# Root columns interleaved with the value tiles, and one GpSimd split placed behind the first column

## The chip, the cores and the metric

The kernel runs on one core of one Trainium2 chip. Five engines work in it, each through its own list of instructions in order: PE (TensorE, matmuls; its weight loads are shown apart as PEld), DVE (VectorE), ACT (ScalarE), POOL (GpSimd) and SP (SyncE, which here only issues DMAs). They wait for one another by counting semaphores that the kernel places by hand. The metric is the device time of one execution in microseconds (us); lower is better.

## What is computed

One decoder block on 512 tokens of width 1024. The part that matters here is its beginning:

```python
h    = rms_norm(x, g_mix)                # x / sqrt(mean(x*x) + eps) * g
proj = h @ w_in                          # q_a,k_a,v_a | q_b,k_b,v_b | gate_a,gate_b
qa = rms_norm(heads(qa), q_norm_a); ka = rms_norm(heads(ka), k_norm_a)   # each of 64 columns
va = heads(va)                           # no norm of its own
```

Behind it stand block-sparse attention with 8 heads, sliding-window attention with 8 heads, two sigmoid gates, an output projection with residual, and a squared-relu feed-forward part.

## The kernel before

**Exact products from parts.** Every fp32 operand is split in a high part (fp32r) and a low part, the difference. A product of two such operands takes three matmuls: high by high, high by low, low by high. The weights come as slabs of 128 x 1024. For slab g, a DMA fills `w_raw`, ACT copies it to `w_hi` (`split_hi`, L624), POOL subtracts to get `w_lo` (`split_lo`, L534) and raises `w_lo_ready`, and PE then uses both. `w_hi` and `w_lo` have two places each, so the split of slab g+2 waits on PE's last use of slab g (`slab_done`).

**The value tiles.** The first four slabs hold the weights of v_a. PE computes them with tokens on partitions (L1476), into four accumulator banks, one for each 128 tokens (`va_tile(r)`, r = 0 to 3). These banks have to be scaled by 1 / rms of the token. That root is computed as a row that is equal on all partitions (`r_all`, 128 x 512), while the value tiles need it as a column, one value to a partition. `x_mean_square` on DVE ends with four `tensor_tensor_reduce` instructions (L1010): each multiplies 128 columns of `r_all` by the identity and sums, which leaves column r in `r_col`, and raises `r_col_ready`. In the profile each is a CUSTOM_DVE_ANT_0 and a DVE_READ_ACCUMULATOR2_ANT. Then ACT writes the scaled high part of tile r from its bank (`va_hi(r)`, L696), and DVE the low part (`va_lo(r)`, L1016), which needs `va_hi(r)`.

**What comes next.** The slabs 4 to 17 are the q and k slabs (13 of them) and v_b. PE does slab g into one of five banks in turn, `acc(g)`: 8 times three matmuls (L1375 to L1377). Slab 4 uses the free fifth bank. Slab 5 uses the bank of value tile 0, so before it PE waits for `w_lo_ready` of slab 5 and for `va_lo(0)`. Behind the matmuls of slab g stands the norm sum of slab g-1 (`head_norm_sum`, two matmuls, L1403 and L1404). It needs the squares of `acc(g-1)`: ACT writes them twice, as high part and in full (`qkv_square`, L660 and L661), and DVE subtracts to get their low part (`qk_split_squares`, L996). The bank's mean is read by DVE (`qk_mean`, L1027).

**Order around the change.** On ACT: `split_hi(5)`, the four `va_hi`, `split_hi(6)`, the squares of slab 4, `split_hi(7)`, and so on. On DVE: the root, the four columns, the four `va_lo`, then L996 of slab 4, L1027 of slab 4, L996 of slab 5. On POOL: `split_lo` of slabs 4, 5, 6, 7, then `split_lo` and `qk_split_lo` (L542) in turn.

Of the kernel before, what the change touches and what calls it, by code (L numbers as in the profile page):

```python
# [32 lines left out]
P = 128  # L33
KT = D // P
QT = S // P
# [56 lines left out]
def build(nc, x_t, slabs, params, table, onehot, tab_dram, out):  # L92
    F32, R = mybir.dt.float32, mybir.dt.float32r
    ALU, ACT = mybir.AluOpType, mybir.ActivationFunctionType
    ctx = ExitStack()
    with ctx:
        def sb(name, shape, dt):
            return ctx.enter_context(nc.sbuf_tensor(name, shape, dt))
# [7 lines left out]
        def sem(name):  # L106
            return ctx.enter_context(nc.semaphore(name))
# [24 lines left out]
        r_all = sb("r_all", [P, S], F32)  # L132
        ident = sb("ident", [P, P], F32)
# [6 lines left out]
        r_col = softmax[:, 0, 0:QT]  # L140
        diagonal = store[:, 12, 0:P]
# [81 lines left out]
        r_col_ready = sem("r_col_ready")  # L223
# [36 lines left out]
        def qk_count(slab):  # L260

            return sum(kind in "qk" for kind in QKV_KIND[:slab])
# [26 lines left out]
        def key_tiles(i, qt):  # L289

            nk = min(2, qt + 1) if i < 8 else qt + 1
            return qt + 1 - nk, nk
# [3 lines left out]
        def units(step):  # L296

            p, qt = step // QT, QT - 1 - step % QT
            return [(2 * step + e, 2 * p + e, e, qt) for e in range(2)]
# [219 lines left out]
        @block.gpsimd  # L519
        def _(pool):  # L520
            pool.memset(ident[:, :], 0.0).then_inc(ident_ready, 1)
            pool.wait_ge(ident_ready, 1)
            pool.affine_select(out=ident[:, :], in_=ident[:, :], compare_op=ALU.not_equal, fill=1.0,
                               base=0, pattern=[[-1, P]], channel_multiplier=1).then_inc(ident_ready, 1)

            pool.wait_ge(arrived[0], 16)
            pool.wait_ge(w_hi_ready, 1)
            pool.tensor_scalar(w_hi[:, 0, FIRST * P:D], w_raw[:, 0, FIRST * P:D], 1.0, 0.0,
                               ALU.mult, ALU.add).then_inc(w_hi_ready, 1)

            def split_lo(g, count):

                pool.wait_ge(w_hi_ready, count)
                pool.tensor_tensor(w_lo[:, g % WS, :], w_raw[:, g % RAW, :],  # L534
                                   w_hi[:, g % WS, :].bitcast(F32), ALU.subtract).then_inc(w_lo_ready, 1)


            def qk_split_lo(g):

                t, n = QKV_TILE[g], qk_count(g)  # L540
                pool.wait_ge(qk_hi_ready, n + 1)
                pool.tensor_tensor(qk_lo[:, t, :], pre[n % 2], qk_hi[:, t, :].bitcast(F32),  # L542
                                   ALU.subtract).then_inc(qk_lo_ready, 1)

            def normalise(step):

                for u, i, e, qt in units(step):
                    n = P * key_tiles(i, qt)[1]
                    pool.wait_ge(rec_ready, step + 1)
                    pool.tensor_scalar(probs[:, u % 4, 0:n], probs[:, u % 4, 0:n], rec[:, u % 8:u % 8 + 1], 1.0,  # L550
                                       ALU.mult, ALU.mult).then_inc(probs_ready, 1)

            def y_lo(p):

                pool.wait_ge(y_hi_ready, p + 1)
                pool.tensor_tensor(qk_lo[:, y_tile(p), :], y_both[:, :], qk_hi[:, y_tile(p), :].bitcast(F32),
                                   ALU.subtract).then_inc(y_lo_ready, 1)

            pool.wait_ge(w_lo_ready, 3)
            for s in range(4, G_GATE + 2):  # L560
                split_lo(s, s + 3)

                if s - 4 >= N_VA:
                    qk_split_lo(s - 4)
            for step in range(STEPS + 1):
                if step >= 1:
                    normalise(step - 1)
                if step == 4:
                    qk_split_lo(LAST_Q)
                if step >= 3 and step % 2:  # L570
                    s = G_GATE + 2 + (step - 3) // 2
                    split_lo(s, s + 3)
                if step >= 8 and step % 4 == 0:
                    y_lo(step // 4 - 2)
            split_lo(G_BRANCH + 1, G_BRANCH + 4)
            split_lo(LATE + 1, LATE + 4)
            for g in range(LATE + 2, G_FF + 3):
                split_lo(g, g + 3)

            def up_lo(j, c):  # L580

                split_lo(G_FF + j, c * TILES + (G_FF + j + 3))

            def down_lo(k, c):

                from_, high, low = unit_at(k, c)
                pool.wait_ge(unit_hi_ready, unit_count(k, c))
                pool.tensor_tensor(low, from_, high.bitcast(F32), ALU.subtract).then_inc(b_lo_ready, 1)

            def chunk_lows(c):  # L590

                down_lo(0, c)
                up_lo(3, c)
                up_lo(4, c)
                down_lo(3, c)
                up_lo(5, c)
                up_lo(6, c)
                down_lo(5, c)

            def last_lows(c):  # L600

                down_lo(0, c)
                up_lo(3, c)
                pool.wait_ge(s_ready, c * 4 + 4)
                down_lo(2, c)
                pool.wait_ge(u_lo_ready, u_count(2, c))
                down_lo(3, c)
                down_lo(4, c)
                pool.wait_ge(u_lo_ready, u_count(3, c))
                down_lo(5, c)  # L610

            with pool.Fori(0, CHUNKS - 1) as c:
                chunk_lows(c)
            last_lows(CHUNKS - 1)

        @block.scalar
        def _(act):
# [19 lines left out]
            for k in range(KT):  # L637
                if k == 0:
                    hi_part(0, slice(0, FIRST * P), first_arrived[0])
                if k == 4:  # L640
# [5 lines left out]
                               scale=par[:, C_MIX + k:C_MIX + k + 1]).then_inc(x_hi_ready, 1)  # L646
# [45 lines left out]
            def va_hi(r):  # L692

                act.wait_ge(slab_done, N_VA)
                act.wait_ge(r_col_ready, QT)
                act.activation(va_hi_part[r], va_tile(r), ACT.Copy,  # L696
                               scale=r_col[:, r:r + 1]).then_inc(va_hi_ready, 1)

# [5 lines left out]
            for r in range(QT):  # L704
                va_hi(r)
# [100 lines left out]
            for n in range(N_OUT):  # L806
# [3 lines left out]
                               scale=par[:, C_FFN + n:C_FFN + n + 1]).then_inc(x1_hi_ready, 1)  # L810
# [107 lines left out]
        def _(dve):  # L918
# [30 lines left out]
            for k in range(KT):  # L949
# [4 lines left out]
                if k == 4:  # L954
# [4 lines left out]
                                         scalar=par[:, C_MIX + k:C_MIX + k + 1],  # L959
                                         in1=x_hi[:, k, :].bitcast(F32), op0=ALU.mult,  # L960
                                         op1=ALU.subtract).then_inc(x_lo_ready, 1)
# [37 lines left out]
            def x_mean_square():  # L999
                dve.wait_ge(ms_done, 1)  # L1000
                dve.tensor_scalar(r_inv_sq, bank[5][:, :], EPS, None, ALU.add).then_inc(ms_ready, 1)
                dve.wait_ge(r_root_ready, 3)
                refine(r_all[:, :], r_root, r_root_sq, r_inv_sq, r_ready, 2)
                dve.wait_ge(ident_ready, 2)
                dve.wait_ge(r_ready, 2)
                dve.wait_ge(xsum_lo_ready, 1)
                for r in range(QT):
                    if r:
                        dve.wait_ge(r_col_ready, r)
                    dve.tensor_tensor_reduce(out=diagonal, in0=r_all[:, P * r:P * r + P], in1=ident[:, :], scale=1.0,  # L1010
                                             scalar=0.0, op0=ALU.mult, op1=ALU.add,
                                             accum_out=r_col[:, r:r + 1]).then_inc(r_col_ready, 1)

            def va_lo(r):
                dve.wait_ge(va_hi_ready, r + 1)
                dve.scalar_tensor_tensor(out=va_lo_part[r], in0=va_tile(r), scalar=r_col[:, r:r + 1],  # L1016
                                         in1=va_hi_part[r].bitcast(F32), op0=ALU.mult,
                                         op1=ALU.subtract).then_inc(va_lo_ready, 1)
# [50 lines left out]

            x_mean_square()  # L1070
            for r in range(QT):
                va_lo(r)
            for g in range(N_VA, N_QKV):
                if g in (10, 11):
# [104 lines left out]
            for n in range(N_OUT):  # L1179
# [7 lines left out]
                                         scalar=par[:, C_FFN + n:C_FFN + n + 1],  # L1187
                                         in1=qk_hi[:, n, :].bitcast(F32), op0=ALU.mult,
                                         op1=ALU.subtract).then_inc(x1_lo_ready, 1)
# [156 lines left out]
            for m in range(2):  # L1346
# [6 lines left out]
                                     in1=to[:, part], op0=ALU.mult, op1=ALU.add).then_inc(rest_sum_ready, 1)  # L1353
# [5 lines left out]
            for h, part in enumerate(HALVES):  # L1359
# [3 lines left out]
                else:  # L1363
                    dve.wait_ge(half_done, 1)
                dve.scalar_tensor_tensor(out=to[:, part], in0=product[:, part], scalar=factor(2, 1), in1=to[:, part],
                                         op0=ALU.mult, op1=ALU.add).then_inc(out_ready, 1)
# [450 lines left out]
```

## Time and profile before

| what | us |
|---|---|
| median of 3 runs | 677.76 |
| lowest and highest | 677.14, 677.97 |
| span of the profiled execution | 674.9 |
| PE busy | 668.8 (99%) |
| DVE busy | 504.8 (75%) |
| ACT busy | 370.2 (55%) |
| POOL busy | 322.9 (48%) |

The span reaches from the first to the last instruction. The profile gives no other time for its execution; the median of the runs is 2.9 us above its span, which lies outside of the first and last instruction. "Busy" is time in which the engine worked on at least one instruction; PE's ends are modelled from the pipeline, so the start times of its rows tell more than the durations. The mean granted TensorE clock over the span is 1.000 of full.

### The profile page before, as it was taken

Reading aid. Unit: us, or ns where it says so; the run is one execution under the profiler, and the core shown is the slowest. Engines: PE = TensorE matmul, PEld = TensorE weight load, DVE = VectorE, ACT = ScalarE, POOL = GpSimd, SP = SyncE. Lnnn points to the kernel's source line nnn. Section 1 sums busy time; section 2 is a strip of 40 time slices with the busy share of each in tenths; the row PEclk is TensorE's granted clock in tenths of the full one; section 3 lists DMA queues with packets and bytes.
Section 4 is the critical chain, followed back from the end, with each engine's and each line's share of the span. In section 5 each row is a group of like instructions: output and inputs, shape, how many; then the busy total and the mean of one; then the engine's idle time right before and its main releaser. Section 6 shows DMA issues by size and latency. Waiting matters only on the chain.

```text
span 674.9 us, 9472 instructions
## 1 busy us (share of the span) xinstructions
PE 668.8 (99%) x3238; PEld 553.7 (82%) x3238; DVE 504.8 (75%) x701; ACT 370.2 (55%) x662; POOL 322.9 (48%) x194
## 2 busy tenths in 40 slices
PE   9999999999999999999999999999999999999998
PEld 7878787788888888888888888888888888888886
DVE  6667898555555555785559879788797888978897
ACT  7467676676665566543347546254463525536360
POOL 0246676456556653444446436246352454435532
PEclk9999999999999999999999999999999999999999
DMA  8222242222232213555222232414132151220303
GB/s 320 95 93 94 76 128 82 78 81 93 96 94 75 71 45 113 157 181 188 82 93 93 100 118 65 153 62 154 64 113 104 62 186 62 93 101 25 125 0 125
DMA packets 22909, 69.87 MB, mean 104 GB/s; under 512 B 2731, under 2 KB 4011, under 8 KB 22876
## 3 DMA queue, kind: packets, MB, share of 16 engines
q1 hardware_dynamic: 22588, 68.92, 30.3%
q10 hardware_dynamic: 288, 0.52, 0.2%
q8 instruction: 19, 0.31, 0.2%
q14 instruction: 14, 0.11, 0.1%
HBM read 67.27 MB, written 2.16 MB: 103 GB/s over the span
## 4 chain that ended last, share of the span: by engine, by line
PE 94%; DVE 2%; ACT 2%; issue 1%; DMA 1%; POOL 0%; SPq 0%; DVEq 0%; ACTq 0%
PE bank L1375 20%; PE bank L1377 20%; PE bank L1376 20%; PE bank L1692 8%; PE bank L1689 8%; PE bank L1691 8%; PE bank L1476 3%; PE bank L1538 2%; PE bank L1525 2%; PE bank L1559 1%; PE bank L1561 1%; DMA store<-x_t 1%; PE bank L1661 1%; DVE store L1010 0%; PE bank L1404 0%
## 5 line engine op out<-in xcount | busy, mean ns | idle before, releaser
L534 POOL TENSOR_TENSOR w_lo<-w_raw,w_hi 128x1024 fp32r<-128x1024 f32 x77 | 190.2, 2474 | 232.7 <-ACT w_hi L624 232.7
L1375 PE MATMUL bank<-qk_hi,w_hi 128*128 128x512 f32 x320 | 125.0, 391 | 0.0
L1377 PE MATMUL bank<-qk_hi,w_lo 128*128 128x512 f32 x320 | 124.5, 389 | 0.0
L1376 PE MATMUL bank<-qk_lo,w_hi 128*128 128x512 f32 x320 | 124.5, 389 | 0.0
L1375 PE MATMUL bank<-x_hi,w_hi 128*128 128x512 f32 x304 | 122.4, 403 | 1.6 <-DVE v_parts L1016 1.1
L1377 PE MATMUL bank<-x_hi,w_lo 128*128 128x512 f32 x304 | 118.8, 391 | 0.0
L1376 PE MATMUL bank<-x_lo,w_hi 128*128 128x512 f32 x304 | 118.4, 389 | 0.0
L624 ACT ACTIVATE w_hi<-w_raw 128x1024 fp32r<-128x1024 f32 x80 | 83.9, 1056 | 59.4 <-PE bank L1377 55.0
L1258 DVE SCALAR_TENSOR_TENSOR store<-bank,softmax,store 128x512 f32<-128x512 f32 x101 | 72.0, 744 | 23.2 <-PE bank L1692 23.1
L1692 PE MATMUL bank<-v_parts,x_lo 128*128 128x512 f32 (+1 forms) x218 | 84.4, 387 | 0.0
L1689 PE MATMUL bank<-v_parts,x_hi 128*128 128x512 f32 (+1 forms) x218 | 84.4, 387 | 0.0
L1377 PEld LDWEIGHTS bank<-qk_hi,w_lo 128*128 128x128 f32 x320 | 60.1, 188 | 12.6
L1375 PEld LDWEIGHTS bank<-qk_hi,w_hi 128*128 128x128 f32 x320 | 60.1, 188 | 12.4 <-DVE w_lo L1169 0.2
L1376 PEld LDWEIGHTS bank<-qk_lo,w_hi 128*128 128x128 f32 x320 | 60.1, 188 | 12.3
L1375 PEld LDWEIGHTS bank<-x_hi,w_hi 128*128 128x128 f32 x304 | 57.1, 188 | 13.8 <-issue 2.9
L1377 PEld LDWEIGHTS bank<-x_hi,w_lo 128*128 128x128 f32 x304 | 57.0, 188 | 12.5
L1376 PEld LDWEIGHTS bank<-x_lo,w_hi 128*128 128x128 f32 x304 | 57.2, 188 | 10.8
L550 POOL TENSOR_SCALAR probs<-probs,softmax 128x256 f32<-128x256 f32 (+3 forms) x64 | 31.3, 502 | 58.8 <-DVE softmax L1106 58.8
L1111 DVE TENSOR_TENSOR pt_lo<-bank,pt_hi 128x256 fp32r<-128x256 f32 (+3 forms) x64 | 27.9, 439 | 35.8 <-ACT pt_hi L747 35.5
L836 ACT ACTIVATE v_parts<-qk_lo_again 128x1024 fp32r<-128x1024 f32 x21 | 21.5, 1056 | 56.2 <-DVE qk_lo_again L1201 44.9
L1692 PEld LDWEIGHTS bank<-v_parts,x_lo 128*128 128x128 f32 x218 | 40.9, 188 | 8.4
L1689 PEld LDWEIGHTS bank<-v_parts,x_hi 128*128 128x128 f32 x218 | 40.9, 188 | 8.3
(165 smaller groups left out, 1213.1 us busy)
## 6 DMA issues: line engine op xcount, KB each, us to landing
w_raw<-slabs SPq DMA_DIRECT2D x80, 512.0 KB, 3.3
bias_m<-slabs SPq DMA_DIRECT2D x16, 512.0 KB, 3.6
qk_hi_again<-slabs SPq DMA_DIRECT2D x16, 512.0 KB, 5.2
store<-x_t SPq DMA_DIRECT2D x16, 256.0 KB, 3.4
bias_m<-tab_dram SPq DMA_DIRECT2D x8, 256.0 KB, 4.3
out<-store SPq DMA_DIRECT2D x7, 256.0 KB, 2.1
bias_m<-tab_dram SPq DMA_DIRECT2D x8, 128.0 KB, 3.6
w_raw<-slabs ACTq DMA_DIRECT2D x2, 256.0 KB, 3.4
```

The source lines that it names most:

```text
L534: pool.tensor_tensor(w_lo[:, g % WS, :], w_raw[:, g % RAW, :], w_hi[:, g % WS, :].bitcast(F32), ALU.subtract).then_inc(w_lo_ready, 1)
L550: pool.tensor_scalar(probs[:, u % 4, 0:n], probs[:, u % 4, 0:n], rec[:, u % 8:u % 8 + 1], 1.0, ALU.mult, ALU.mult).then_inc(probs_ready, 1)
L624: act.activation(w_hi[:, g % WS, :], w_raw[:, g % RAW, :], ACT.Copy).then_inc(w_hi_ready, 1)
L836: act.activation(high, from_, ACT.Copy).then_inc(unit_hi_ready, 1)
L1111: dve.tensor_tensor(pt_lo[:, slot(u), keys], bank[5 + e][:, keys], pt_hi[:, slot(u), keys].bitcast(F32), ALU.subtract).then_inc(pt_lo_read ...
L1258: dve.scalar_tensor_tensor(out=to, in0=product, scalar=factor(j, m), in1=to, op0=ALU.mult, op1=ALU.add).then_inc(ready, 1)
L1375: pe.matmul(out_, wh, xh, start=first, stop=False)
L1376: pe.matmul(out_, wh, xl, start=False, stop=False)
L1377: last = pe.matmul(out_, wl, xh, start=False, stop=end)
L1689: pe.matmul(to, u_high, high[:, p, cols], start=(opens and p == 0), stop=False, skip_group_check=True)
L1691: pe.matmul(to, u_high, low[:, p, cols], start=False, stop=False, skip_group_check=True)
L1692: last = pe.matmul(to, u_low, high[:, p, cols], start=False, stop=(p == 1), skip_group_check=True)
```

## The change

Three things. In DVE's list, `r_column(r)` is cut out of `x_mean_square` and stands ahead of `va_lo(r)` in the loop over tiles. ACT's `va_hi(r)` waits for r+1 columns and no longer for all four. POOL's `split_lo(5)` waits for the first column.

```diff
--- before
+++ after
@@ gpsimd @@
             pool.wait_ge(w_lo_ready, 3)
             for s in range(4, G_GATE + 2):
+                if s == 5:
+                    pool.wait_ge(r_col_ready, 1)
                 split_lo(s, s + 3)
@@ scalar @@
             def va_hi(r):
                 act.wait_ge(slab_done, N_VA)
-                act.wait_ge(r_col_ready, QT)
+                act.wait_ge(r_col_ready, r + 1)
@@ vector @@
                 dve.wait_ge(xsum_lo_ready, 1)
-                for r in range(QT):
-                    if r:
-                        dve.wait_ge(r_col_ready, r)
-                    dve.tensor_tensor_reduce(... accum_out=r_col[:, r:r + 1]).then_inc(r_col_ready, 1)
+
+            def r_column(r):
+
+                if r:
+                    dve.wait_ge(r_col_ready, r)
+                dve.tensor_tensor_reduce(... accum_out=r_col[:, r:r + 1]).then_inc(r_col_ready, 1)
@@ vector @@
             x_mean_square()
             for r in range(QT):
+                r_column(r)
                 va_lo(r)
```

DVE's list before, from the end of the root to the first squares of a q or k slab. An ISA row that writes `store` is a column's reduction, the one that writes `softmax` alone its read of the sum; bank0, 1, 2 and 6 are the value tiles 0 to 3.

```order
L984 SCALAR_TENSOR_TENSOR r_all<-store 128x512 [waits r_root_ready]
L987 SCALAR_TENSOR_TENSOR r_all<-r_all,store 128x512 [waits r_ready]
L1010 ISA store,softmax<-r_all,ident 128x128 [waits xsum_lo_ready,r_ready,ident_ready]
L1010 ISA softmax 128x1
L1010 ISA store,softmax<-r_all,ident 128x128 [waits r_col_ready]
...
L1016 SCALAR_TENSOR_TENSOR v_parts<-bank0,softmax,v_parts 128x8x64 [waits va_hi_ready]
L1016 SCALAR_TENSOR_TENSOR v_parts<-bank1,softmax,v_parts 128x8x64 [waits va_hi_ready]
L1016 SCALAR_TENSOR_TENSOR v_parts<-bank2,softmax,v_parts 128x8x64 [waits va_hi_ready]
L1016 SCALAR_TENSOR_TENSOR v_parts<-bank6,softmax,v_parts 128x8x64 [waits va_hi_ready]
L996 TENSOR_TENSOR pt_lo<-store,pt_hi 128x512 [waits sq_ready]
```

The same stretch of DVE's list now:

```order
L1014 ISA store,softmax<-r_all,ident 128x128 [waits xsum_lo_ready,r_ready,ident_ready]
L1014 ISA softmax 128x1
L1020 SCALAR_TENSOR_TENSOR v_parts<-bank0,softmax,v_parts 128x8x64 [waits va_hi_ready]
L1014 ISA store,softmax<-r_all,ident 128x128 [waits r_col_ready]
...
L1020 SCALAR_TENSOR_TENSOR v_parts<-bank1,softmax,v_parts 128x8x64 [waits va_hi_ready]
...
L1020 SCALAR_TENSOR_TENSOR v_parts<-bank6,softmax,v_parts 128x8x64 [waits va_hi_ready]
L998 TENSOR_TENSOR pt_lo<-store,pt_hi 128x512 [waits sq_ready]
```

The four columns stood in a row ahead of the four low parts; each of the last three columns now stands behind the low part of the tile before it, and with it behind that tile's wait for ACT.

POOL's list at its splits of slabs 4 to 7, as a difference:

```order
 L528 TENSOR_SCALAR w_hi<-w_raw 128x512 [waits w_hi_ready,slab_arrived0]
 L534 TENSOR_TENSOR w_lo<-w_raw,w_hi 128x1024 [waits w_hi_ready,w_lo_ready]
-L534 TENSOR_TENSOR w_lo<-w_raw,w_hi 128x1024 [waits w_hi_ready] x4
+L534 TENSOR_TENSOR w_lo<-w_raw,w_hi 128x1024 [waits w_hi_ready,r_col_ready]
+L534 TENSOR_TENSOR w_lo<-w_raw,w_hi 128x1024 [waits w_hi_ready] x3
 L542 TENSOR_TENSOR qk_lo<-store,qk_hi 128x512 [waits qk_hi_ready]
```

Nothing moved there; the second split of the four, slab 5's, has one wait more. The lists of PE and ACT hold the same instructions in the same order, and SP's list is unchanged.

## Rows read from the trace of the kernel before

**Rows 1.** The page, part 1: busy us, share of the span, count.

```profile
PE 668.8 (99%) x3238; PEld 553.7 (82%) x3238; DVE 504.8 (75%) x701; ACT 370.2 (55%) x662; POOL 322.9 (48%) x194
```

**Rows 2.** Waits of PE: who waited for whom, total us, times, longest us.

```profile
PE bank L1375 <- DVE v_parts L1016: 1.1, 1, 1.1
```

**Rows 3.** Timeline of DVE: start, duration, line, operation, count, [idle before <- releaser].

```profile
30.55 2.27 DVE L1010 CUSTOM_DVE_ANT_0 store<-r_all,ident 128x128 f32<-128x128 f32 x1
...
32.86 0.29 DVE L1010 CUSTOM_DVE_ANT_0 store<-r_all,ident 128x128 f32<-128x128 f32 x1
33.08 0.08 DVE L1010 DVE_READ_ACCUMULATOR2_ANT softmax<- 128x1 f32 x1
...
33.75 0.08 DVE L1010 DVE_READ_ACCUMULATOR2_ANT softmax<- 128x1 f32 x1
34.65 2.73 DVE L1016 SCALAR_TENSOR_TENSOR v_parts<-bank,softmax,v_parts 128x512 fp32r<-128x512 f32 x4 [0.81 <-ACT v_parts L696]
38.31 2.01 DVE L996 TENSOR_TENSOR pt_lo<-store,pt_hi 128x512 fp32r<-128x512 f32 x1 [0.93 <-ACT store L661]
```

**Rows 4.** Timeline of POOL.

```profile
30.23 2.45 POOL L534 TENSOR_TENSOR w_lo<-w_raw,w_hi 128x1024 fp32r<-128x1024 f32 x1 [3.47 <-ACT w_hi L624]
37.38 2.39 POOL L534 TENSOR_TENSOR w_lo<-w_raw,w_hi 128x1024 fp32r<-128x1024 f32 x1 [4.71 <-ACT w_hi L624]
...
48.38 2.41 POOL L534 TENSOR_TENSOR w_lo<-w_raw,w_hi 128x1024 fp32r<-128x1024 f32 x1 [3.47 <-ACT w_hi L624]
50.75 1.74 POOL L542 TENSOR_TENSOR qk_lo<-store,qk_hi 128x512 fp32r<-128x512 f32 x1
...
60.17 2.41 POOL L534 TENSOR_TENSOR w_lo<-w_raw,w_hi 128x1024 fp32r<-128x1024 f32 x1 [1.79 <-ACT w_hi L624]
...
117.60 1.29 POOL L542 TENSOR_TENSOR qk_lo<-store,qk_hi 128x512 fp32r<-128x512 f32 x1
```

**Rows 5.** Timeline of DVE, two further instructions that ran beside POOL.

```profile
49.31 2.03 DVE L996 TENSOR_TENSOR pt_lo<-store,pt_hi 128x512 fp32r<-128x512 f32 x1 [0.98 <-ACT store L661]
...
60.83 0.68 DVE L1027 SCALAR_TENSOR_TENSOR store<-store,bank 128x512 f32<-128x512 f32 x1
```

**Rows 6.** Timeline of ACT.

```profile
29.09 1.06 ACT L624 ACTIVATE w_hi<-w_raw 128x1024 fp32r<-128x1024 f32 x1
33.93 2.42 ACT L696 ACTIVATE v_parts<-bank,softmax 128x512 fp32r<-128x512 f32 x4 [3.78 <-DVE softmax L1010]
36.23 1.08 ACT L624 ACTIVATE w_hi<-w_raw 128x1024 fp32r<-128x1024 f32 x1
...
37.65 0.62 ACT L661 ACTIVATE store<-bank 128x512 f32<-128x512 f32 x1
```

**Rows 7.** Timeline of PE around slab 5 (matmuls).

```profile
34.04 0.39 PE L1377 MATMUL bank<-x_hi,w_lo 128*128 128x512 f32 x1
35.55 0.47 PE L1375 MATMUL bank<-x_hi,w_hi 128*128 128x512 f32 x1 [1.12 <-DVE v_parts L1016]
35.85 0.40 PE L1376 MATMUL bank<-x_lo,w_hi 128*128 128x512 f32 x1
36.09 0.39 PE L1377 MATMUL bank<-x_hi,w_lo 128*128 128x512 f32 x1
...
41.09 0.39 PE L1403 MATMUL bank<-pt_hi,pt_lo 128*128 128x512 f32 x1
...
41.54 0.39 PE L1375 MATMUL bank<-x_hi,w_hi 128*128 128x512 f32 x1
```

**Rows 8.** Timeline of PE in the first 10 us.

```profile
0.93 4.63 PE L1450 MATMUL bank<-ones 128*128 128x128 f32 x20 [0.93 <-DVE ones L919]
5.91 1.68 PE L1476 MATMUL bank<-w_hi,x_hi 128*128 128x512 f32 x4 [0.34 <-ACT x_hi L645]
7.43 1.08 PE L1476 MATMUL bank<-w_lo,x_hi 128*128 128x512 f32 x4
```

**Rows 9.** One window: busy us of each engine (count), granted clock, DMA share, GB/s.

```profile
34.00:42.00 8.00, 6.88 (x31) 5.37 (x31) 5.00 (x6) 4.93 (x8) 2.39 (x1) 1.00 0.30 101
```

More of the change, by code:

```diff
@@ L1006, in x_mean_square @@
                 dve.wait_ge(xsum_lo_ready, 1)
-                for r in range(QT):
-                    if r:
-                        dve.wait_ge(r_col_ready, r)
-                    dve.tensor_tensor_reduce(out=diagonal, in0=r_all[:, P * r:P * r + P], in1=ident[:, :], scale=1.0,
-                                             scalar=0.0, op0=ALU.mult, op1=ALU.add,
-                                             accum_out=r_col[:, r:r + 1]).then_inc(r_col_ready, 1)
+            def r_column(r):
+                if r:
+                    dve.wait_ge(r_col_ready, r)
+                dve.tensor_tensor_reduce(out=diagonal, in0=r_all[:, P * r:P * r + P], in1=ident[:, :], scale=1.0,
+                                         scalar=0.0, op0=ALU.mult, op1=ALU.add,
+                                         accum_out=r_col[:, r:r + 1]).then_inc(r_col_ready, 1)
             def va_lo(r):
```

## The prediction

> **What bounds the kernel now.** I read the busy shares first: PE is busy 99% of the span [rows 1]. So an edit to DVE, ACT and POOL moves the time only where PE waits for them. The list of PE's waits, read second, has one entry that belongs to the edited lines: PE stood 1.1 us ahead of slab 5 until `va_lo(0)` was done [rows 2]. Everything else in this stretch must be judged by how close it is to making PE wait. For that I laid the timelines of the four engines from 28 to 42 us beside each other.
>
> **Why PE waits there.** ACT had slab 5's high part at 29.09 + 1.06 = 30.15, and POOL began its low part at 30.23 [rows 4, 6]. DVE began the first column at 30.55. That reduction lasted 2.27 us, the next one, of the same form, 0.29 [rows 3]. It ended at 32.82, which is 0.14 behind POOL's end (30.23 + 2.45 = 32.68). The same pattern stands at L996: its two sources lie in SBUF, it began at 38.31 inside POOL's work of 37.38 to 39.77 and ended at 40.32, 0.55 behind it [rows 3, 4]; once more, 49.31 + 2.03 = 51.34 against POOL's 48.38 + 2.41 = 50.79, again 0.55 [rows 4, 5]. L1027, with one source in SBUF and one in a bank, took 0.68 wholly inside POOL's 60.17 to 62.58 [rows 4, 5]. I read this as: a DVE instruction with two SBUF sources waits for the running POOL instruction and then does its own work (0.14 us for 128 columns, 0.55 for 512); one that reads a bank does not wait.
>
> The Trainium skill names such a lock (SBUF — State Buffer, section "Who interferes with whom"): with two SBUF inputs DVE contends with a GpSimd instruction that reads SBUF, and whoever comes first keeps the port for its whole instruction. It speaks of instruction classes and not of this custom reduction. Its rule gives the first column 0.29 us once POOL is held back, and also speaks against the change, since column 1 then meets POOL; a cost of first use, the rival below, would leave the 2.27 us where they are.
>
> **What the change removes.** POOL now starts behind column 0, so column 0 should take 0.29 us: its sum is read out at about 30.55 + 0.30 = 30.85 (0.30 from the start of a reduction to the end of its read, 32.86 to 33.16 in [rows 3]). ACT started `va_hi(0)` 0.10 behind the last read (33.83 to 33.93) and DVE `va_lo(0)` 0.72 later (34.65) [rows 3, 6]. So `va_hi(0)` starts at 30.95, `va_lo(0)` at 31.67 and is over by 32.4. POOL starts slab 5's low part 0.08 behind its release, as it did behind ACT (30.15 to 30.23), at 30.93, and with 2.45 us ends at 33.38. PE's last matmul of slab 4 starts at 34.04 and the next could start 0.23 later, at 34.27 [rows 7]. Both conditions of slab 5 are met by then, with 0.9 us to spare. The stall of 1.12 us goes, and with it the slow restart: the steps behind it were 0.30 and 0.24 us where the steady one is 0.227 (22 steps from 36.09 to 41.09), so 0.09 more. Slab 5's 24 matmuls then end, and the norm sum of slab 4 could start, at 34.27 + 24 x 0.227 = 39.71, against 41.09 before: **1.38 us earlier**. This would be the whole gain.
>
> **What is late next.** The columns 1 to 3 are no longer free. DVE goes from `va_lo(0)` to column 1 at 31.67 + 0.66 = 32.33 (four `va_lo` in 2.73 us: steps of 0.66). POOL is now in slab 5's low part until 33.38, so column 1 waits: it ends at 33.38 + 0.14 and is read by 33.53. From there each round is a relay between two engines: 0.10 to ACT, 0.72 to `va_lo`, 0.66 to the next column, 0.30 to its read, 1.78 us in all. Column 2 is read at 35.31, column 3 at 37.09, `va_hi(3)` starts at 37.19. Before, ACT started `split_hi(6)` at 36.23; its four `va_hi` ran in a row from 33.93 to 36.35, so the last began near 35.66, 0.57 before [rows 6]. Now `split_hi(6)` starts at 37.19 + 0.57 = **37.76, later by 1.53 us**.
>
> Behind it, in ACT's order, stand the squares of slab 4, and behind these PE's norm sum. Before: `split_hi(6)` 36.23, POOL's split of slab 6 37.38 (1.15 later) to 39.77, the square L661 37.65 (1.42 later), L996 38.31 (0.66 behind that), its end 40.32. PE came to the norm sum at 41.09 and did not wait; a release takes 0.16 to reach PE (`va_lo(0)` 34.65 + 0.74 = 35.39, PE 35.55), so 41.09 - 40.48 = 0.6 us was the slack [rows 3, 4, 6, 7]. Now: POOL has slab 6 from 38.91 to 41.30, L661 starts at 39.18, L996 starts at 39.84, inside POOL's instruction, and ends at 41.30 + 0.55 = 41.85. PE can start the norm sum at **42.01**. It gets there at 39.71 and stands for 2.3 us.
>
> **The sum.** The norm sum is at 42.01 against 41.09, +0.92; the slow restart, 0.09, moves with the stall, and adds as PE goes on to slab 6: 41.54 becomes 42.55, **+1.0 us**. So one stall of 1.12 us is traded for one of 2.3 us. It doesn't come back later: slab 6's low part is ready at 41.30 and `va_lo(1)` at 34.3 + 0.8 = 35.1, both before PE needs them; ACT's `split_hi(7)` waits on PE's last use of slab 5, which comes earlier, so POOL has slab 7's low part by some 44.2, where PE needs it at 42.55 + 26 x 0.227 = 48.5. From slab 6 on the other engines wait for PE in each slab, and the program is as before, only shifted. SP's loads are behind `w_lo_ready` of four slabs before: slab 9's and slab 10's loads go out 0.7 and 1.5 us later, and ACT takes these slabs up only behind PE's slabs 7 and 8, some 20 us on at 26 x 0.227 = 5.9 us a slab, so they cost nothing. The added POOL wait costs nothing beyond the shift counted: behind it only the split of slab 6 is queued, which waits for ACT longer. The span becomes 675.9; with the 2.9 us outside, from the median 677.76, the time is **678.8 us**, +0.15%. That is inside the 0.2% (1.4 us) which a measurement of this kernel can just tell from none.
>
> **Rivals.**
>
> *Column 1 isn't held up* (a short reduction slips in, or POOL starts late enough). Then column 1 starts at 32.33 and is read by 32.63, all behind it is 0.90 earlier, L996 ends at 40.95, PE starts the norm sum at 41.11 instead of 41.09, with the restart 0.1 later than before: 677.9. Against it: each of the three two-SBUF instructions above waited to POOL's end. Chance 0.12.
>
> *The 2.27 us are the first use of the custom reduction*, not POOL. It is the first such instruction of the program, so the row alone fits both. Then POOL's split of slab 5 is pushed to 32.9, ends at 35.4, and every step above is 1.98 later: +3.0, 680.8. Against it stands that it ended 0.14 behind POOL, as the lock asks. Chance 0.06.
>
> *POOL goes first at 41.30.* L996 waits for slab 6's low part, and POOL's slab 7 part is released by ACT by then. If POOL takes it up ahead of L996, that one waits a further 2.4: +3.4, 681.2. Against it: at 50.79 POOL had its next instruction ready, and DVE went first; that POOL instruction took 1.74 us where a lone one took 1.29, 0.45 of waiting [rows 4, 5]. Chance 0.05.
>
> *The clock falls.* Over the window with the 1.12 us stall the granted clock stayed 1.00 [rows 9]; no longer stall is in the trace, and the new one is twice that. At the start PE ran at the lower level: four matmuls took 1.68 us, the next four 1.08 [rows 8], 0.6 lost. If the lower level lasted as long as from PE's first matmul to there (0.93 to 7.43, 6.5 us), half of it would be lost, 3.2. So +1.6 to +4.2: 679.4 to 682.0. Chance 0.09. The Trainium skill (TensorE: Matmul & The Clock Gate, "What's actually happening") says that idleness halves TensorE's clock until activity releases it; the trace's stall of 1.12 us did not do this.
>
> *The gain stays.* If L996 were not held (POOL and DVE not in each other's way) and ACT's relay shorter than I reckon, PE reaches the norm sum unhindered: -1.4, 676.4. It needs L996's end by 39.55, while its start alone is at 39.84, or 38.94 with column 1 free. Chance 0.06.
>
> **How the numbers follow.** My forecast, the traded stall, has 0.62 and its own range 678.1 to 679.6 (0.3 us on the relay's hand-offs, 0.4 on a median). The range 677.2 to 681.0 takes in the forecast, the free column, the first use and the lower half of the clock's case, about 0.82. Slower by over 0.2% (above 679.1): a quarter of the forecast, 0.15, first use 0.06, POOL first 0.05, clock 0.08: 0.34. Faster by over 0.2%: most of the last rival, 0.05. The rest, 0.61, is within.
>
> **What would show it.** In the changed kernel's timeline: the first L1014 reduction at 0.29 us, POOL's L534 right behind it at about 30.9, the second reduction at over 1 us; no wait of PE ahead of slab 5 and a wait of about 2.3 us on L998's product ahead of the norm sum, now L1408; ACT's `split_hi(6)` near 37.8. The forecast is wrong if PE's list of waits has nothing at the norm sum, if the first reduction stays above 2 us, or if matmuls behind the stall step at 0.43 us.

## The result, and the profile after

| | before | changed |
|---|---|---|
| median, 15 runs each | 676.92 us | 679.07 us |
| lowest and highest | 676.23, 678.87 | 676.88, 680.54 |
| ratio | | 1.0021, 95% interval 1.0011 to 1.0031 |
| span of the profiled execution | 674.9 us | 675.9 us |
| TensorE clock, mean of each run | 0.999 or 1.000 in all of the 72 runs taken beside the experiments | 0.999 or 1.000 in 8 runs, 0.996 or 0.997 in 7 |

The changed kernel is slower by 0.2%, 1.4 us with an interval of 0.7 to 2.1. The plain difference of the two medians is larger, 2.15 us; I go by the ratio and its interval. The profiled execution of it, at clock 1.000, has the span of the forecast, 675.9 us. The median is a little above the forecast's 678.8, and inside the range.

PE's list of waits in the changed kernel (who waited for whom, total us, times, longest):

```profile
PE bank L1408 <- DVE pt_lo L998: 2.0, 1, 2.0
```

The wait ahead of slab 5 [rows 2] is gone, and one at the norm sum has come. DVE's timeline shows why; it answers to [rows 3]:

```profile
30.62 0.29 DVE L1014 CUSTOM_DVE_ANT_0 store<-r_all,ident 128x128 f32<-128x128 f32 x1
...
31.74 0.75 DVE L1020 SCALAR_TENSOR_TENSOR v_parts<-bank,softmax,v_parts 128x512 fp32r<-128x512 f32 x1 [0.82 <-ACT v_parts L698]
32.41 1.15 DVE L1014 CUSTOM_DVE_ANT_0 store<-r_all,ident 128x128 f32<-128x128 f32 x1
33.49 0.08 DVE L1014 DVE_READ_ACCUMULATOR2_ANT softmax<- 128x1 f32 x1
34.38 0.75 DVE L1020 SCALAR_TENSOR_TENSOR v_parts<-bank,softmax,v_parts 128x512 fp32r<-128x512 f32 x1 [0.82 <-ACT v_parts L698]
35.05 0.28 DVE L1014 CUSTOM_DVE_ANT_0 store<-r_all,ident 128x128 f32<-128x128 f32 x1
...
37.03 0.08 DVE L1014 DVE_READ_ACCUMULATOR2_ANT softmax<- 128x1 f32 x1
37.93 0.75 DVE L1020 SCALAR_TENSOR_TENSOR v_parts<-bank,softmax,v_parts 128x512 fp32r<-128x512 f32 x1 [0.82 <-ACT v_parts L698]
39.85 1.99 DVE L998 TENSOR_TENSOR pt_lo<-store,pt_hi 128x512 fp32r<-128x512 f32 x1 [1.17 <-ACT store L663]
```

The first column takes 0.29 us, the second meets GpSimd and takes 1.15, and the low parts come one by one, 0.82 us of waiting for ACT ahead of each, where they stood in one row of four before. ACT gets to its copy of slab 6 late by that, at 37.80 where it was 36.23:

```profile
37.80 1.05 ACT L626 ACTIVATE w_hi<-w_raw 128x1024 fp32r<-128x1024 f32 x1
```

GpSimd's timeline, which answers to [rows 4]:

```profile
31.00 2.41 POOL L534 TENSOR_TENSOR w_lo<-w_raw,w_hi 128x1024 fp32r<-128x1024 f32 x1 [4.17 <-DVE softmax L1014]
38.93 5.17 POOL L534 TENSOR_TENSOR w_lo<-w_raw,w_hi 128x1024 fp32r<-128x1024 f32 x2 [5.51 <-ACT w_hi L626]
```

Slab 6's low part starts at 38.93 where it started at 37.38. L998 came at 39.85, inside it, and ended at 41.84. The two GpSimd instructions in a row took 5.17 us where twice 2.41 is 4.82: the second waited for L998. PE's timeline, which answers to [rows 7]:

```profile
39.55 0.39 PE L1382 MATMUL bank<-x_hi,w_lo 128*128 128x512 f32 x1
41.90 0.50 PE L1408 MATMUL bank<-pt_hi,pt_lo 128*128 128x512 f32 x1 [1.96 <-DVE pt_lo L998]
42.23 0.39 PE L1409 MATMUL bank<-pt_lo 128*128 128x512 f32 x1
42.47 0.40 PE L1380 MATMUL bank<-x_hi,w_hi 128*128 128x512 f32 x1
```

From the first column's start to slab 6's first matmul it is 42.47 - 30.62 = 11.85 us, before it was 41.54 - 30.55 = 10.99: **0.86 us later**. This difference, "column to slab 6", is what I compare the experiments by. It leaves out what happens ahead of the columns, where the start of an execution varies by half a us and more with the arrival of x.

### The profile page after: what moved, and what is told of

It reads as the page before. It is cut to its first block, busy times and chain, and to the rows that moved or that the text cites. A ratio compares the mean times of both kernels' runs of the same rounds, so it can differ in the third digit from the quotient of the medians.

```text
span 675.9 us, 9473 instructions
## 1 busy us (share of the span) xinstructions
PE 668.9 (99%) x3238; PEld 553.7 (82%) x3238; DVE 503.0 (74%) x701; ACT 370.8 (55%) x662; POOL 323.6 (48%) x194
## 4 chain that ended last, share of the span: by engine, by line
PE 93%; ACT 2%; DVE 2%; issue 1%; DMA 1%; POOL 0%; SPq 0%; ACTq 0%; DVEq 0%
PE bank L1380 20%; PE bank L1382 20%; PE bank L1381 20%; PE bank L1694 8%; PE bank L1697 8%; PE bank L1696 8%; PE bank L1481 3%; PE bank L1543 2%; PE bank L1530 2%; PE bank L1564 1%; PE bank L1566 1%; DMA store<-x_t 1%; PE bank L1666 1%; PE bank L1408 0%; PE bank L1409 0%
```

## The experiments

### The changed kernel again, and with its stall filled

The first question was the part of the 1.4 us that the 0.9 of the trace does not give. Two kernels ran on one chip: the changed kernel itself, and the changed kernel with work of no use in the stall:

```diff
+FILL = 9
...
+                    if (g, kt) == (5, KT - 1):
+                        for _ in range(FILL):
+                            pe.matmul(bank[4][:, :], x_hi[:, 0, 0:P], x_hi[:, 1, :], start=True, stop=True)
                     if (g, kt) in AFTER:
```

> The changed kernel once more, to see its runs with their spans and granted clocks beside those of the kernel before. Theory A (only the traded stall, PE waits 2.0 us at the norm sum in the place of 1.1 us ahead of slab 5): all runs lie about 1.0 us over the kernel before, ratio 1.0015, and the mean granted clock is 1.000 in each. Theory B (the longer stall also lets TensorE's clock fall in part of the runs): runs at 1.000 lie 1.0 us over before, and runs at about 0.997 lie some 2 us higher still (0.003 of 676 us is 2.0), ratio 1.002 to 1.003.

> The changed kernel, with nine more matmuls of 512 columns (their result is not used) on PE between slab 5 and the norm sum of slab 4: 9 x 0.227 = 2.04 us of work in the place of the 1.96 us that PE stands there. No other engine's work changes. Both theories: the norm sum still starts near 41.9 us and the profile's span stays at 675.9 us, within 0.2. Theory A: the timed runs are as the changed kernel's, ratio to it within 0.05%. Theory B: with the stall filled the granted clock is 1.000 in every run and the median falls by 1 to 1.5 us against the changed kernel, to 1.0 us over before.

Measured: the kernel before 677.65 us on this chip; the changed kernel 679.48, ratio to before 1.0028 (1.0016 to 1.0040), 2 of its 6 runs at a mean clock of 0.997, these two with a median of 679.86, the four at 1.000 with 679.04. In the first table the eight runs at 0.999 or more have a median of 678.2, 1.3 us over before, and the seven lower ones 679.6. So a lower mean clock adds some 0.8 to 1.4 us to the runs that have it, less than the 2 of Theory B. With the stall filled it is 677.44, ratio 1.0002 (0.9994 to 1.0011), all 12 runs at 0.999 or 1.000. PE's timeline with the stall filled:

```profile
39.26 2.20 PE L1511 MATMUL bank<-x_hi 128*128 128x512 f32 x9
41.42 0.50 PE L1409 MATMUL bank<-pt_hi,pt_lo 128*128 128x512 f32 x1
41.76 0.40 PE L1410 MATMUL bank<-pt_lo 128*128 128x512 f32 x1
41.99 0.39 PE L1381 MATMUL bank<-x_hi,w_hi 128*128 128x512 f32 x1
```

The first column starts at 30.10 there, 0.5 us earlier than in the profile of the changed kernel, and the span, 675.5, is shorter by about as much. Column to slab 6 is 11.89 us: the program is as late as the changed kernel, 0.90 over before, and still its runs are 2.0 us shorter than the changed kernel's in the median, where Theory B had 1 to 1.5, and level with before where it had 1.0 over. PE did nothing more useful in that time; it was only not idle. The part of this that the runs name is the clock: no run with the stall filled shows a mean below 0.999. The lower means alone, though, stand in fewer than half of the changed kernel's runs, and so don't carry 2.0 us.

### The new order without GpSimd's wait

```diff
             for s in range(4, G_GATE + 2):
-                if s == 5:
-                    pool.wait_ge(r_col_ready, 1)
                 split_lo(s, s + 3)
```

> The changed kernel without GpSimd's new wait: columns interleaved with the tiles, GpSimd takes slab 5's low part at 30.2 us as before. My relay: column 0 is held to GpSimd's end and read at 32.83, columns 1 to 3 free at 34.61, 36.39, 38.17; ACT's slab 6 copy at 38.84, GpSimd's slab 6 part 39.99 to 42.39, the low squares of slab 4 end at 42.94, PE's norm sum at 43.1. So PE waits about 0.3 us ahead of slab 5 and 3.0 us at the norm sum, and slab 6 starts 2.1 us later than before: span 677.0. A rival, that the hold-up is counted once in either order and the two are alike, gives 675.9. If the clock falls with a longer stall, the runs at a lower clock are more than in the changed kernel, and their median is above 679.5.

Measured: 681.06 us, ratio to before 1.0051 (1.0033 to 1.0069), 5 of 6 runs at 0.994 to 0.997; profiled span 679.2. PE's timeline, and then three windows of 2 us (busy us of PE, PEld, DVE, ACT and POOL with counts, granted clock, DMA share, GB/s):

```profile
42.35 0.80 PE L1406 MATMUL bank<-pt_hi,pt_lo 128*128 128x512 f32 x1 [2.65 <-DVE pt_lo L996]
42.95 0.63 PE L1407 MATMUL bank<-pt_lo 128*128 128x512 f32 x1
43.37 0.63 PE L1378 MATMUL bank<-x_hi,w_hi 128*128 128x512 f32 x1
...
48.06 0.62 PE L1380 MATMUL bank<-x_hi,w_lo 128*128 128x512 f32 x1
48.49 0.43 PE L1378 MATMUL bank<-x_hi,w_hi 128*128 128x512 f32 x1
48.76 0.40 PE L1379 MATMUL bank<-x_lo,w_hi 128*128 128x512 f32 x1
```

```profile
40.00:42.00 2.00, 0.00 (x0) 0.00 (x0) 1.68 (x1) 2.00 (x4) 2.00 (x2) 0.93 0.00 0
42.00:44.00 2.00, 1.65 (x4) 1.36 (x5) 0.69 (x2) 0.21 (x1) 2.00 (x1) 0.50 0.58 190
...
46.00:48.00 2.00, 2.00 (x6) 1.59 (x5) 1.61 (x3) 0.28 (x1) 0.00 (x0) 0.50 0.51 195
```

After 2.65 us of idleness the granted clock is 0.50, the 1.2 GHz level, and a matmul steps on every 0.43 us in the place of 0.227. It is 14 steps from 42.35 to 48.49, 6.14 us where 14 x 0.227 is 3.18: 3.0 us lost, restart included. The relay itself came out as reckoned: the first column took 2.27 us, the norm sum started 42.35 - 29.99 = 12.36 us behind the first column, 1.82 over the 10.54 of before (2.0 was forecast). That the first column is back at 2.27 us with GpSimd's wait taken out, and was 0.29 with it in, ties its length to GpSimd; the rival by which the two orders cost the same has fallen. This is the clearest view of the rival that I had priced at 0.6 to 3.2 us and given a chance of 0.09.

### GpSimd behind all four columns, columns in a row

The kernel before with two lines:

```diff
             for s in range(4, G_GATE + 2):
+                if s == 5:
+                    pool.wait_ge(r_col_ready, 4)
                 split_lo(s, s + 3)
```

> The kernel before with one edit: GpSimd takes slab 5's low part behind all four columns; the columns stay in a row. The four columns then take 0.34 each and are read by 31.9; ACT's four parts run from 32.0, GpSimd's slab 5 part from 32.0 to 34.4, PE starts slab 5 at 34.5 (0.25 us of waiting in the place of 1.12). ACT's slab 6 copy is then bound by PE's end of slab 4, 34.5, GpSimd's slab 6 part ends at 38.1, the low squares of slab 4 at 38.7, well ahead of PE's norm sum at 40.0. So the whole program is 1.0 us earlier: span 673.9, ratio 0.9985. The rival, that slab 5's low part coming later costs as much as the held column, gives 674.9.

Measured: 676.48 us, ratio to before 0.9986 (0.9977 to 0.9995), clock 1.000 in all 11 runs, span 673.3 (673.9 was forecast; the first column came 0.7 us earlier than in the profile of before). DVE's, GpSimd's and PE's timelines:

```profile
29.85 0.29 DVE L1012 CUSTOM_DVE_ANT_0 store<-r_all,ident 128x128 f32<-128x128 f32 x1
...
30.86 0.29 DVE L1012 CUSTOM_DVE_ANT_0 store<-r_all,ident 128x128 f32<-128x128 f32 x1
31.07 0.08 DVE L1012 DVE_READ_ACCUMULATOR2_ANT softmax<- 128x1 f32 x1
31.97 2.73 DVE L1018 SCALAR_TENSOR_TENSOR v_parts<-bank,softmax,v_parts 128x512 fp32r<-128x512 f32 x4 [0.82 <-ACT v_parts L698]
```

```profile
31.24 2.40 POOL L534 TENSOR_TENSOR w_lo<-w_raw,w_hi 128x1024 fp32r<-128x1024 f32 x1 [4.95 <-DVE softmax L1012]
```

```profile
33.69 0.50 PE L1377 MATMUL bank<-x_hi,w_hi 128*128 128x512 f32 x1
...
39.72 0.39 PE L1377 MATMUL bank<-x_hi,w_hi 128*128 128x512 f32 x1
```

All four columns are read 1.3 us behind the start of the first. GpSimd comes at 31.24 and hinders none of them; PE stands some 0.1 us ahead of slab 5. Column to slab 6 is 39.72 - 29.85 = 9.87 us, 1.12 less than before. The same wait that the change adds for one column pays when it stands behind four, with the columns left together.

### GpSimd's wait for one column alone

The same two lines with `1` in the place of `4`.

> The kernel before with GpSimd's wait alone: slab 5's low part behind the first column, the four columns in a row and ACT waiting for all four, as before. Column 0 takes 0.29 us. GpSimd is released 0.08 behind its read, when DVE has just begun column 1 (0.11 behind the read), so the engines meet between columns. Theory D (a waiting instruction gets the port before the next one of the engine that just had it, as at 50.79 us in the profile before): GpSimd goes in behind column 1, columns 2 and 3 wait 2.4 us, the last read is at 34.1 against 33.83 before, and the program is 0.2 us later: span 675.1, ratio 1.000 to 1.001. Rival (DVE keeps the port for its row of columns): all four are read by 32, as in four_columns, and the program gains 1.0 us: 673.9, ratio 0.9985.

Measured: 677.93 us against 677.54, ratio 1.0006 (0.9994 to 1.0017); span 676.2, where 675.1 was forecast, about 1 us more, which comes up again at the end of the experiments. DVE's, GpSimd's and PE's timelines:

```profile
30.04 0.29 DVE L1012 CUSTOM_DVE_ANT_0 store<-r_all,ident 128x128 f32<-128x128 f32 x1
...
30.37 0.29 DVE L1012 CUSTOM_DVE_ANT_0 store<-r_all,ident 128x128 f32<-128x128 f32 x1
...
30.71 2.36 DVE L1012 CUSTOM_DVE_ANT_0 store<-r_all,ident 128x128 f32<-128x128 f32 x1
```

```profile
30.42 2.50 POOL L534 TENSOR_TENSOR w_lo<-w_raw,w_hi 128x1024 fp32r<-128x1024 f32 x1 [3.92 <-DVE softmax L1012]
```

```profile
35.12 0.47 PE L1377 MATMUL bank<-x_hi,w_hi 128*128 128x512 f32 x1 [1.21 <-DVE v_parts L1018]
```

GpSimd went in between columns 1 and 2, and column 2 took the 2.3 us that column 0 took before. PE waits 1.2 us ahead of slab 5 and slab 6 starts 41.12 - 30.04 = 11.08 us behind the first column, 0.1 later than before. The engine that waits gets in at the next gap, as expected; the wait alone moves the hold-up from one column to another.

### The squares ahead of slab 6's copy

The changed kernel with ACT's `qkv_square(4)` put ahead of `split_hi(6)`:

```diff
             for g in range(N_VA, N_QKV):
+                if g == 4:
+                    qkv_square(g)
                 split_hi(g + 2)
...
-                if not is_v(g):
+                if not is_v(g) and g > 4:
                     qkv_square(g)
```

> The changed kernel with ACT's two squares of slab 4 ahead of its copy of slab 6. Then DVE's L998 starts near 38.9, before GpSimd has slab 6, takes 0.69 and the norm sum follows at 39.8 without a wait. If GpSimd's hold on L998 were what costs the 2.0 us, the program would gain them. My sum says that slab 6's low part is late by nearly as much: ACT's copy 38.8 to 39.8, GpSimd 39.9 to 42.3, PE at 42.45 on slab 6 where the changed kernel had 42.47. So the 2.0 us wait moves from the norm sum to slab 6 and nothing is gained: span 675.9 at clock 1.000.

Measured: 678.65 us against 677.54, ratio 1.0013 (1.0003 to 1.0022), 4 of 10 runs at 0.997; span 676.8. DVE's low squares and PE:

```profile
38.22 0.69 DVE L1000 TENSOR_TENSOR pt_lo<-store,pt_hi 128x512 fp32r<-128x512 f32 x1 [0.22 <-ACT store L663]
```

```profile
39.31 0.39 PE L1411 MATMUL bank<-pt_lo 128*128 128x512 f32 x1
41.62 0.50 PE L1382 MATMUL bank<-x_hi,w_hi 128*128 128x512 f32 x1 [1.92 <-POOL w_lo L534]
```

The low squares take 0.69 us, and PE waits 1.92 us for GpSimd's low part of slab 6 instead. Column to slab 6 is 41.62 - 29.93 = 11.69, 0.70 over before. So with GpSimd's hold on the squares gone, only 0.16 us is won. The test is not a clean one, as the squares in front make the copy of slab 6 later themselves; but in the kernel before and in the one with GpSimd behind four columns L996 and L998 were held just as long (2.01 and 2.02 us), and PE did not wait for them. What costs is the relay that makes ACT late for both of its jobs, the squares and slab 6. The granted clock fell to 0.5 in this profile too, three matmuls behind the restart: nine steps, from 42.42 to 46.07, took 3.65 us where 9 x 0.227 is 2.04, 1.6 us lost. The span is yet only 0.9 over the 675.9 that I had written for clock 1.000, because the first column started 0.7 us earlier than in the changed kernel's profile.

### The start, and the two edits together

In the second profile of the changed kernel (span 678.5 us) PE waited 1.33 us at the mean square, which no other profile shows:

```profile
24.22 2.85 DVE L982 TENSOR_TENSOR pt_hi<-store,pt_hi 128x512 fp32r<-128x512 f32 x1
```

```profile
24.15 2.37 POOL L534 TENSOR_TENSOR w_lo<-w_raw,w_hi 128x1024 fp32r<-128x1024 f32 x1 [18.37 <-ACT w_hi L626]
```

It is the same meeting, at slab 4. To keep it out, one line puts slab 4's low part behind the last step of the sum of squares:

```diff
             pool.wait_ge(w_lo_ready, 3)
+            pool.wait_ge(xsum_lo_ready, 1)
```

This line went into the kernel before, the changed kernel, the one with the stall filled, and the one with GpSimd behind four columns.

> The kernel before, with GpSimd's low part of slab 4 put behind DVE's x_sum_lo (the last step of the sum of squares, two SBUF sources). In a profiled execution of the changed kernel that step met GpSimd's slab 4 part by a hair (24.22 against 24.15), lasted 2.85 us and made PE wait 1.33 us at the mean square; in the profile of before it was over first (23.19). Theory C (this chance meeting at the start makes the two groups of times that the kernel before shows, near 676.5 and 677.8): no run has it any more, the runs lie in one group at 676.2 to 677.0, median about 0.7 us under before where half of its runs are in the upper group. Rival (the two groups come from elsewhere): ratio within 0.03% of before, groups unchanged.

> The changed kernel with the same edit at the start. If the change's own cost is the traded stall plus a clock that falls in part of the runs, this lies over before_start by 1.0 us in the runs at clock 1.000 and by some 3 us in those at 0.997: median 1.0 to 3.0 us over before_start.

> The changed kernel with the edit at the start and the nine unused matmuls in the stall ahead of the norm sum. With the start's lottery taken out, the traded stall alone is left: 0.9 to 1.0 us over before_start (ratio between the two 1.0014), clock 1.000 in all runs. The first filled kernel came out at 1.0002 of before, less than the 1.0015 of this sum; if the sum is wrong, this one will be level with before_start again.

> The kernel before with GpSimd's slab 4 part behind x_sum_lo and its slab 5 part behind all four columns (columns in a row, as before): both edits keep GpSimd off a DVE step that PE waits for. 1.0 us from slab 5, and what before_start brings: about 675.3, ratio to before 0.997 to 0.998, and the lowest of all.

| kernel, with the line at the start | us, median | ratio to before (677.39) | runs at 0.997 |
|---|---|---|---|
| before | 677.85 | 1.0008 (0.9997 to 1.0020) | 0 of 12 |
| changed | 678.90 | 1.0026 (1.0014 to 1.0037) | 4 of 8 |
| changed, stall filled | 677.09 | 1.0000 (0.9991 to 1.0009) | 0 of 11 |
| behind four columns | 675.45 | 0.9972 (0.9961 to 0.9983) | 0 of 8 |

My theory on the start fell: the kernel before gained nothing by the line, and its runs spread as before, from 676.48 to 678.32 with one at 680.82. The meeting at slab 4 is real, but it stands in one of the eight profiles taken without the line, too rare to make the spread. The changed kernel with the line is 1.05 us over the kernel before with it, inside the 1.0 to 3.0 forecast; with the stall filled it is 0.8 under it, where 0.9 to 1.0 over was forecast. The last kernel met its forecast of 675.3 in number, though the part of it that the line was to bring isn't there. The changed kernel's profile of this set has the clock's fall at the changed kernel's own stall. PE's timeline and two windows:

```profile
41.38 0.50 PE L1409 MATMUL bank<-pt_hi,pt_lo 128*128 128x512 f32 x1 [1.96 <-DVE pt_lo L999]
...
42.18 0.49 PE L1382 MATMUL bank<-x_lo,w_hi 128*128 128x512 f32 x1
...
42.89 0.63 PE L1381 MATMUL bank<-x_hi,w_hi 128*128 128x512 f32 x1
43.32 0.63 PE L1382 MATMUL bank<-x_lo,w_hi 128*128 128x512 f32 x1
...
45.83 0.40 PE L1382 MATMUL bank<-x_lo,w_hi 128*128 128x512 f32 x1
```

```profile
42.00:44.00 2.00, 2.00 (x7) 1.56 (x6) 1.86 (x2) 1.10 (x2) 1.58 (x1) 0.59 0.58 225
44.00:46.00 2.00, 2.00 (x6) 1.57 (x6) 1.24 (x3) 0.79 (x2) 0.00 (x0) 0.56 0.71 205
```

The stall is 1.96 us, as in the profile above that stayed at 1.00; here the clock fell about 1 us behind the restart (the mean of 0.59 over 42 to 44 puts the step near 42.4). From 42.18 to 45.83 it is nine steps, 3.65 us where 9 x 0.227 is 2.04: 1.6 us lost.

The last kernel is the fastest of all: 0.28% under the kernel before. In its profile column to slab 6 is 39.96 - 30.10 = 9.86 us, 1.13 less than before. The interval runs from 1.15 to 2.6 us less; the trace's 1.13 lies at its edge, and the median's 1.9 us is more than the trace gives.

**One source of the spread of the runs** shows in that same profile, whose execution (676.48 us) was the slowest of its kernel's 8; the other seven lie from 675.05 to 675.48. DVE near the end, in the last chunk of the feed-forward part, and GpSimd beside it:

```profile
636.35 1.23 DVE L1204 TENSOR_TENSOR qk_lo_again<-qk_hi_again,qk_lo_again 128x1024 f32<-128x1024 f32 x1 [1.75 <-DMA qk_hi_again<-slabs]
637.49 3.43 DVE L1208 TENSOR_TENSOR bias_m<-qk_hi_again,bias_m 128x1024 f32<-128x1024 f32 x1
```

```profile
636.66 3.18 POOL L534 TENSOR_TENSOR w_lo<-w_raw,w_hi 128x1024 fp32r<-128x1024 f32 x1 [3.47 <-ACT w_hi L627]
```

```profile
654.55 0.47 PE L1692 MATMUL bank<-w_hi,x_hi 128*128 128x512 f32 x1 [0.52 <-issue]
```

DVE had waited 1.75 us for a DMA; in the profile of 673.3 us above it waited 0.97, began L1207 before GpSimd came, and that step took 1.22. Here the step fell behind GpSimd and took 3.43. It is a third place of the same meeting, decided by when one DMA lands, and PE waits twice behind it, 0.8 us in all. Three of the twelve profiles (this one, the second of the changed kernel and that of the wait alone) show DVE waiting 1.66 us or more for this DMA, and in all three a step of DVE then falls behind GpSimd. From slab 6's first matmul to the end of the span it is 634.7 to 635.1 us in these three, and 633.3 to 633.8 in the six others whose clock stayed at 1.00: the meeting costs 0.9 to 1.8 us. The two groups in which the runs of the kernel before lie, near 676.5 and 677.8, are about as far apart; that this meeting makes them isn't shown, since a timed run leaves no trace. I have not tried to take it out.

## Why the prediction was right, point by point

- **The bound.** Right: only PE's waits counted, and the change replaced one by another.
- **Column 0 without GpSimd: 0.29 us.** Measured 0.29. It is also the first use of the custom reduction, so the rival that blamed the first use has fallen; so has the one by which column 1 isn't held, since it took 1.15 us.
- **The relay.** Forecast: column 1 read at 33.53, `va_hi(3)` 37.19, `split_hi(6)` 37.76, the low squares 39.84 to 41.85. Measured, with the first column 0.07 later than before: read at 33.57, ACT's copy of slab 6 at 37.80, the low squares 39.85 to 41.84. The round of 1.78 us was measured at 1.77 (two rounds from 33.49 to 37.03 between reads).
- **Who goes first at GpSimd's end.** Right: DVE, and GpSimd's slab 7 part waited 0.35 us. With L998 held and the relay as long as forecast, the rival by which the gain stays has fallen too. The kernel with the wait alone shows the mirror image, GpSimd going in ahead of DVE's next column.
- **The stall, 2.3 us.** By the forecast's own count, from the start that was possible to the one that was made, it is 41.90 - (39.55 + 0.23) = 2.1 us; the profile counts 1.96 from a matmul's end. The release took 0.06 us (41.84 to 41.90) and not 0.16 to reach PE, and GpSimd's slab 5 part 2.41 and not 2.45. These are most of the 0.15 by which the sum of 1.0 was over the 0.86 of the trace.
- **The time.** The mechanism and the difference were right, +1.0 us forecast and +1.4 (0.7 to 2.1) measured. That the median came within 0.3 us of the forecast 678.8 is in part luck. The forecast started from 677.76, a median of three runs; fifteen give 676.92. And the 2.9 us that it put outside the span are the median of those three runs less the span of another execution: in every run on record with its span, the time is 1.7 to 1.9 us above it. So the profiled execution of the kernel before took about 674.9 + 1.8 = 676.7, and the sum for one like it is 675.9 + 1.8 = 677.7, which is what the profiled one of the changed kernel took (677.71). The median lies 1.4 us above that, by what the sum left out: the clock, and the delays at the end of the program. One miss nearly made up for the other.
- **The clock, chance 0.09.** This is the term that was mis-sized. The price held, 0.6 to 3.2 us on top: about 1.6 behind a stall of 2.0 us and 3.0 behind one of 2.65. But it had been read from rows that don't show it: the granted clock at the start of the kernel before is at full,

```profile
0.00:10.00 10.00, 8.72 (x36) 7.70 (x37) 5.73 (x18) 6.44 (x9) 1.32 (x7) 1.00 0.80 289
```

and the four matmuls that took 1.68 us there took 1.15 to 1.25 in ten of the other profiles, so it was no lower level that made them long. That the price was still about right is luck. The chance did not hold: a lower mean clock is in 9 of 21 runs of the changed kernel, in 4 of 8 with the line at the start, in 4 of 10 with the squares first (stall of 1.9 us), in 5 of 6 with the longer stall, and in none of the 72 runs of the kernel before taken beside the experiments (stall of 1.1 us), nor in the 23 with the stall filled. I had asked whether the clock falls as if there were one answer; behind the same 1.96 us it fell in one profile and not in two others. The Trainium skill (TensorE: Matmul & The Clock Gate, "What's actually happening") has the two levels, and the steps of 0.43 and 0.227 us agree with them.

**What stays open.** The kernel with the stall filled is 0.90 us late by its trace and level with the kernel before by its ratio (1.0002 and 1.0000). The kernel behind four columns with the line at the start is 1.9 us ahead by its median and 1.1 by its trace; without the line median and trace agree (1.17 and 1.12). The lowest runs narrow it down. Beside the lowest run of the kernel before on the same chip, the lowest behind four columns is 1.10 us less without the line and 1.15 less with it, and the lowest with the stall filled 0.76 and 0.68 over: close to the traces. So the stretch at slab 5 costs what the traces show, and the rest lies in how many executions carry a further delay of a us or so, in runs whose mean clock reads 1.000. The meeting at the end of the program has that size, but that the filled kernels meet it less often wasn't shown. Nor is the changed kernel explained in full: its lowest run is 0.65 us over that of before in the first table, but 2.4 and 1.4 over in the sets of six and eight.

## What to carry to other kernels

When two engines hand small pieces to each other, finishing each piece at once turns one transfer between them into as many as there are pieces. Here rounds of 1.77 us, one for each further piece, replaced one row of columns and one row of parts, and made ACT's next, unrelated job late. If a short row of DVE steps with two SBUF sources is held up by a GpSimd instruction, put that instruction behind the whole row and leave the row together: its wait for one piece only moves the hold-up to the next piece. And price a PE stall not by its length alone: here part of the executions with a stall of 1.9 us or more paid for it again at half the clock, and none with 1.3 us or less. Filling a stall of 2.0 us with work of no use brought the median down by 2.0 us in one pair of kernels and by 1.8 in the other, with the useful work no earlier; how much of that is the clock stays open.

## What the runs showed of the hardware

- A DVE step with two SBUF sources and a GpSimd step with SBUF sources exclude each other, in both directions: 0.29 us became 2.27 (before), 1.15 (changed), 2.36 (the wait alone), and GpSimd's pair 5.17 in the place of 4.82. A DVE step that reads a bank was not held (0.68 us inside GpSimd's 2.41, [rows 4, 5]). A waiting engine gets in at the next gap between two instructions of the other.
- Behind 1.96 us of PE idleness the granted clock stayed at 1.00 in two profiles of the changed kernel and fell to about half in the one with the line at the start; behind 1.92 us it fell in one; behind 2.65 us in one (there it had fallen before PE restarted); behind 1.33 us and less in none of the profiles.
- Behind a stall at full clock PE's first step takes 0.30 to 0.34 us, the second 0.23 or 0.24, the steady one 0.227.
